# Two more weight slots for the mixture of experts, selection matrices in a ring of three, and fewer products ahead of the routing's positions

## What is computed

```python
def hier_moe(x, router_grp, router_exp, w1, w3, w2):
    xt = x.reshape(-1, D_MODEL)                         # 320 tokens, D_MODEL = 1024
    gp, gi = lax.top_k(jax.nn.softmax(xt @ router_grp), 1)          # best of 4 groups
    sel = ...                                           # the 8 experts of that group
    ev, ei = lax.top_k(sel, 2)
    ew = jax.nn.softmax(ev) * gp
    eid = gi * EXP_PER_GROUP + ei
    combine = jnp.sum(jax.nn.one_hot(eid, N_EXPERTS) * ew[..., None], axis=1)
    for e in range(N_EXPERTS):                          # 32
        hid = jax.nn.silu(xt @ w1[e]) * (xt @ w3[e])    # FF = 256
        y = y + combine[:, e:e + 1] * (hid @ w2[e])
...
y = rms_norm(h + y, ln_f)
```

## Time and profile before

| | |
|---|---|
| median of 3 executions | 959.48 us (954.65, 959.48, 965.29) |
| profiled execution, its own time | 955.93 us |
| its span | 954.3 us |
| mean granted TensorE clock | 0.905 of full |
| TensorE busy | 790.9 us (83%) |
| HBM read | 211.29 MB |

### The profile page before, as it was taken

How to read it: one execution, slowest core, us unless ns; L and a number is a source line. 1 busy time by engine, 2 the same in 40 slices (tenths; PEclk the granted TensorE clock), 3 DMA queues, 4 the chain that set the end, 5 groups by cost and what they waited for, 6 DMA issues and landing times. The chain is left out here.

```text
span 954.3 us, 20697 instructions
## 1 busy us (share of the span) xinstructions
PE 790.9 (83%) x8699; PEld 473.0 (50%) x8699; DVE 352.6 (37%) x653; ACT 186.6 (20%) x430; POOL 153.7 (16%) x300
## 2 busy tenths in 40 slices
PE   3999799989689799584867776799959987899985
PEld 2445466656466567452544554575454433344421
DVE  2000522359532354275775661021252213231113
ACT  3003122125321210132111232210112110111102
POOL 8200020043400100130235335112000000000000
PEclk9999899979889799597877889699959998999999
DMA  8522222122312122155899999996316999999993
GB/s 323 205 88 89 88 103 89 45 76 88 99 30 68 54 39 81 52 169 180 302 416 419 416 342 410 363 386 247 108 70 279 424 422 426 395 384 421 424 425 144
DMA packets 49110, 219.20 MB, mean 230 GB/s; under 512 B 17615, under 2 KB 22010, under 8 KB 24442
## 3 DMA queue, kind: packets, MB, share of 16 engines
q1 hardware_dynamic: 41856, 186.23, 50.6%
q0 software_dynamic: 6512, 31.48, 8.5%
q10 hardware_dynamic: 650, 0.18, 0.1%
HBM read 211.29 MB, written 6.57 MB: 228 GB/s over the span
## 5 line engine op out<-in xcount | busy, mean ns | idle before, releaser
L226 PE MATMUL bank<-arena 128*128 128x320 f32 x256 | 82.8, 467 | 4.2 <-PEq L112 4.2
L1456 DVE STREAM_TRANSPOSE arena<-arena 128x2048 f32<-128x2048 f32 x32 | 72.1, 2288 | 9.4 <-DMA arena<-in_ck 8.4
L201 POOL DMA_DIRECT2D arena<-in_cv x112 | 57.8, 516 | 105.9 <-PE bank L1719 75.6
L503 PE MATMUL bank<-arena 128*128 128x336 f32 x224 | 70.9, 472 | 4.2 <-DVE arena L649 4.2
L2259 PE MATMUL bank<-arena 128*32 128x512 f32 x512 | 67.3, 610 | 6.8 <-DMA arena<-in_w_exp 6.1
L2448 DVE TENSOR_TENSOR arena<-arena,bank 128x512 f32<-128x512 f32 x40 | 27.5, 688 | 116.3 <-PE bank L2236 113.3
L1719 PE MATMUL bank<-arena 128*16 128x128 f32 x1024 | 41.0, 326 | 33.3 <-DMA arena<-in_cv 18.0
L482 PE MATMUL bank<-arena 128*128 128x512 f32 (+1 forms) x144 | 62.1, 593 | 0.0
L226 PEld LDWEIGHTS bank<-arena 128*128 128x128 f32 x256 | 48.6, 201 | 25.6 <-issue 9.5
L1678 PE MATMUL bank<-arena 32*32 32x512 f32 x1024 | 46.3, 714 | 18.1 <-DVE arena L1456 8.6
L503 PEld LDWEIGHTS bank<-arena 128*128 128x128 f32 x224 | 43.8, 200 | 27.2 <-issue 9.7
(11 more groups left out here) (463 smaller groups left out, 1091.8 us busy)
## 6 DMA issues: line engine op xcount, KB each, us to landing
arena<-in_w_exp SPq DMA_DIRECT2D x99, 1024.0 KB, 20.5
arena<-in_ck SPq DMA_DIRECT2D x128, 256.0 KB, 6.3
arena<-in_cv POOLq DMA_DIRECT2D x112, 256.0 KB, 8.1
arena<-in_w_gate SPq DMA_DIRECT2D x8, 1024.0 KB, 4.8
arena<-in_w_za SPq DMA_DIRECT2D x7, 1024.0 KB, 6.9
arena<-in_w_zb SPq DMA_DIRECT2D x6, 1024.0 KB, 12.8
arena<-in_cv SPq DMA_DIRECT2D x16, 256.0 KB, 3.5
arena<-in_w_proj SPq DMA_DIRECT2D x4, 1024.0 KB, 20.0
```

The source lines that it names most:

```text
L201: eng.dma_start(tile[n:P:4, :], src[bass.ds(page, 1)].rearrange("a (p j) n -> (a p) (j n)", j=4))\
L226: mm = nc.tensor.matmul(bank[b][:, 0:TM], w[:, k, a, :], xnT[:, k, NMETA:T], start=(k == 0), stop=(k == KT - 1))
L503: mm = nc.tensor.matmul(bank[j % 2][:, 0:T], w[:, k, (j % 2) * P:(j % 2 + 1) * P], xnT[:, k, :], start=(k == 0), stop=(k == KT - 1))
L1456: return nc.vector.transpose(kT[b % 2][:, :, 128 * m:128 * m + 128].rearrange("p j (n k) -> p n j k", n=4), slot[m].rearrange("p (n j k) - ...
```

## The change

`gsel` shrinks to three quads, used in turn, and lies elsewhere; what comes free holds two more weight slots, so `FIRST` becomes 18. Places 16 and 17 of the ring are loaded in the merge block, one after the residual rows are written, one after the normalised rows are. The pair and triangle constants move. `select(q + 2)` waits for quad q - 1's gather. The final norm's rows are loaded into the slot of the fourth expert's part 1 of quad 6, behind a wait for that part's use. The counts of tiles 0 and 1 against the triangle are one product of 64 columns, in all five products, and `cnt_ps` is raised behind them; the totals follow into another PSUM bank with a semaphore of their own.

```diff
-        full = [S(f"slot_full{i}") for i in range(SLOTS + 8)]
+        full = [S(f"slot_full{i}") for i in range(SLOTS + 10)]
...
+        FIRST = len(wslot) + 2
...
-        FIRST = len(wslot)
...
-        pair, tri2 = sp6(P), sp6(P)
+        pair, tri2 = arena[:, free_k - 2 * P:free_k - P], arena[:, free_k - P:free_k]
...
-        gcmp = sp7(MAXOV, NE)
+        gcmp = Space(arena, sp7.at, sp7.hi)(MAXOV, NE)
...
+        gsel = Space(arena, mark7, mark_t + NHT * HALF)(3, NT, P)
+        spw = Space(arena, mark7 + 3 * NT * P, tail - SLOT)
+        late16 = spw(SLOT)
+        late17 = arena[:, tail - 2 * SLOT:tail - SLOT]
+        assert spw.at <= tail - 2 * SLOT
+        wslot += [late16, late17]
...
                     expert_load(sp, 0, 1, j)
+                sp.wait_ge(S("h2_sb"), NHT)
+                expert_load(sp, *ring[FIRST - 2])
+                sp.wait_ge(S("x2_ready"), NT)
+                expert_load(sp, *ring[FIRST - 1])
...
-                for i in range(NT):
-                    for k in range(i + 1):
-                        r = slice(0, TROWS[k])
-                        nc.tensor.matmul(bank[7][:, i * NE:(i + 1) * NE],
-                                         (ones if k < i else tri_tok if k < NT - 1 else tri2)[r, :], fe(k)[r, :],
-                                         start=(k == 0), stop=(k == i))
+                cols = lambda i, n=1: bank[7][:, i * NE:(i + n) * NE]
+                both = pick[:, 0:2].rearrange("p i g e -> p (i g e)")
+                last = slice(0, TROWS[NT - 1])
+                nc.tensor.matmul(cols(0, 2), tri_tok, both, start=True, stop=False)
+                nc.tensor.matmul(cols(2), tri2[last, :], fe(2)[last, :], start=False, stop=False)
+                nc.tensor.matmul(cols(1), ones, fe(0), start=False, stop=False)
+                for k in range(NT - 1):
+                    mm = nc.tensor.matmul(cols(2), ones, fe(k), start=False, stop=(k == NT - 2))
+                mm.then_inc(S("cnt_ps"), 1)
                 for k in range(NT):
                     r = slice(0, TROWS[k])
-                    mm = nc.tensor.matmul(bank[7][:, NT * NE:(NT + 1) * NE], ones[r, :], fe(k)[r, :],
+                    mm = nc.tensor.matmul(bank[6][:, 0:NE], ones[r, :], fe(k)[r, :],
                                           start=(k == 0), stop=(k == NT - 1))
-                mm.then_inc(S("cnt_ps"), 1)
+                mm.then_inc(S("tot_ps"), 1)
...
-                ch(nc.vector.tensor_copy(tot, bank[7][:, NT * NE:(NT + 1) * NE]))
+                dve.wait_ge(S("tot_ps"), 1)
+                ch(nc.vector.tensor_copy(tot, bank[6][:, 0:NE]))
...
-        gsel = Space(arena, mark7, mark_t + NHT * HALF)(NQD, NT, P)
...
+        lnf = wslot[load_slot(NQD - 2, 1, QE - 1)]
+        lnf2, lnf3 = lnf[:, 0:DM], lnf[:, DM:DM + HALF]
...
-                sp.dma_start(lnb2, ln_row[2, :].partition_broadcast(P)).then_inc(S("lnf_in"), 16)
+                sp.wait_ge(S(used[1]), NQD - 1)
+                sp.dma_start(lnf2, ln_row[2, :].partition_broadcast(P)).then_inc(S("lnf_in"), 16)
...
-                    gather(xg[:, q % 2], gsel[:, q], "xg_ps")
+                    gather(xg[:, q % 2], gsel[:, q % 3], "xg_ps")
...
                     if q + 2 < NQD:
+                        if q:
+                            dve.wait_ge(S("xg_ps"), 2 * q)
                         select(q + 2)
```

More of the change, by code:

```diff
@@ L1875, in build @@
         mark7 = sp7.at
-        sp7 = Space(arena, free_o - NPAIR * T, free_k)
+        sp7 = Space(arena, free_o - NPAIR * T, free_k - 2 * P)
         ohg, w4, eg = (sp7(NT, NG) for _ in range(3))
@@ L2184, in build @@
         used = ("w13a_used", "w13b_used")
+        assert ring.index((NQD - 2, 1, QE - 1)) + FIRST >= len(ring)
+        lnf = wslot[load_slot(NQD - 2, 1, QE - 1)]
+        lnf2, lnf3 = lnf[:, 0:DM], lnf[:, DM:DM + HALF]
         ybank = (0, 1, 2, 3, 6)
@@ L2202, in _ @@
                                              .rearrange("a p n -> (a p) n")).then_inc(ofull[part], 16)
-                sp.dma_start(lnb2, ln_row[2, :].partition_broadcast(P)).then_inc(S("lnf_in"), 16)
+                sp.wait_ge(S(used[1]), NQD - 1)
+                sp.dma_start(lnf2, ln_row[2, :].partition_broadcast(P)).then_inc(S("lnf_in"), 16)
                 for r, c in ((UP, slice(0, HALF)), (DN, slice(HALF, DM))):
-                    sp.dma_start(lnb3[r, :], ln_row[2, c].partition_broadcast(P // 2)).then_inc(S("lnf_in"), 16)
+                    sp.dma_start(lnf3[r, :], ln_row[2, c].partition_broadcast(P // 2)).then_inc(S("lnf_in"), 16)
                 for i in range(NT - 1):
@@ L2427, in select @@
                     e4 = slice(QE * q, QE * (q + 1))
-                    v = gsel[:, q].rearrange("p i (e s) -> p i e s", e=QE)
+                    v = gsel[:, q % 3].rearrange("p i (e s) -> p i e s", e=QE)
                     ch(nc.vector.tensor_tensor(v, bc(bc(iot[:, 0:CAP], 1, QE), 1, NT), bc(flat(posm, e4), 3, CAP),
@@ L2537, in result @@
                     nc.vector.scalar_tensor_tensor(out=tile_of(x2, i), in0=tile_of(h2, i), scalar=rstd[:, i:i + 1],
-                                                   in1=lnb2 if i < NT - 1 else lnb3, op0=mult, op1=mult)\
+                                                   in1=lnf2 if i < NT - 1 else lnf3, op0=mult, op1=mult)\
                         .then_inc(S("y_ready"), 1)
```

## The result

The changed kernel takes 951.61 us (median of 20 executions, 947.64 to 956.53) against 960.23 for the kernel before, now also measured 20 times. The ratio is 0.991, its 95% interval 0.9893 to 0.9926: 8.6 us less, 7.1 to 10.3. The forecast was 9.8 us less. The profiled execution took 953.16 us, its span is 951.6. TensorE's busy time (791.4 us, 790.9 before) and the bytes read (211.29 MB) are the same and the mean granted clock is nearly so (0.900, 0.905 before); the time came out of waiting.

The account below looks back on a forecast made before the run. The prediction took the moe block to be bound by its stream of weight loads; 4.9 (two loads) + 3.9 (dent) + 1.0 (routing) = 9.8 us off 957.7 gave 948.0 us, range 941 to 958.

Parts of the forecast that it names:

- The bound: Moe block: bound by its stream of 1 MB weight loads, 83 of them, 2.47 us each.
- Two loads, 4.9 us: Places 16 and 17 load during merge, leaving 81 stream loads; overflow pass and stream end come 4.9 us earlier.
- The dent, 3.9 us: Stream at 831 to 846 us, 314 GB/s: 18 slots keep the queue filled; gain 3.9 us, bounds 0 to 3.9.
- The final norm's rows, which I had put at nothing: Wait ahead of these rows near the end: costs nothing, with 10 us of cover before they are needed.
- Routing, 1.0 us: End of merge: five count products and separate totals start the moe block 1.0 us earlier, range 0.5 to 2.0.
- What follows the last landing ... the change alters none of it.: After the last weight load lands: the remaining 18.4 us stay as they were.
- a tail of more than 18.4 us: Sign of a wrong forecast: over 18.4 us after the last landing, the final norm's rows among its releasers.
- The sum: Whole kernel: 4.9 + 3.9 + 1.0 = 9.8 us less, from 957.7 to about 948.0 us.
- A: Rival: the stream's dent stays or moves, a rate near 314 GB/s in 825 to 850; 951.8 us, chance 0.15.
- B: Rival: the stream doesn't get ahead because TensorE bounds quads 1 to 3; about 955 us, chance 0.1.
- E: Rival: the late merge loads are held, for instance until the barrier, the dent still closes; 953 us, chance 0.06.
- D: Rival: TensorE's clock stays at its lower level through the overflow pass; slower, 971 us, chance 0.04.

Follow-up runs that it names:

- slots_only: The changed kernel with the old nine count products under one semaphore, 18 slots kept; 951.95 us, ratio 0.9904.
- late_in_stream: The changed kernel with places 16 and 17 loaded as the first loads of the moe block's stream; 956.28 us, ratio 0.9952.
- warm_merge: The changed kernel with unread products added: seven between last logits and counts, two ahead of the first gather; 948.62 us, ratio 0.9879.
- counts_only: The kernel before with only the five count products and the totals' own bank and semaphore; 958.32 us, ratio 0.9981.
- one_slot: The changed kernel with 17 slots, only place 16 loaded late in the merge; 954.54 us, ratio 0.9928.
- no_final_rows: The changed kernel without the final norm's three row loads and VectorE's wait for them; 946.97 us, ratio 0.9878.
- rows_late: The changed kernel with the final norm's rows issued only when the first half of outputs(7) is done; 948.21 us, ratio 0.9900.
- rows_late_warm_merge: The changed kernel with the final norm's rows issued behind the stream and unread products filling the merge's end; 949.58 us, ratio 0.9896.

## Why the prediction was right, and where its terms were off

*The bound.* Right. Two waits for weights mark the path in both kernels, and taking loads out of the stream moved the end.

*Two loads, 4.9 us.* Right: 82.3 to 77.3 us up to the overflow pass, 5.0; 77.3 in slots_only, 82.6 where the loads were put back.

*The dent, 3.9 us.* Right in its mechanism, too large by 1.2. In the changed kernel's profile the dent closed fully (422 GB/s) and place 65 came in time, yet the last weights came only 2.7 us earlier behind the overflow pass (2.6 to 3.1 in the profiles of the changed kernel, slots_only, late_in_stream and warm_merge). The step that failed is that the bytes made up in the dent all come back at the last landing. About 1.0 us of them is found in the last 8 us, where the DMA engines are without work for 15% of the time instead of 3%. The final norm's rows, which I had put at nothing because nobody waits for them, have part in it: with them behind the stream the stretch is 127.8, 3.6 less than before. But no run takes them out of the kernel before, so whether they cost more here than there is not shown. That with no pause the 16 engines drift apart, and those ahead move rows while the slowest still has weights, is a guess; no view here shows single engines.

*Routing, 1.0 us.* Right: 0.92 in counts_only, by the way given, the totals. In the changed kernel the ten count instructions took 2.66 us instead of my 2.42 (706.89 to 709.55), and that cost nothing, since the totals came last anyway. That the cost goes little by what is streamed does hold: at the lower clock one of the totals' instructions took 401 ns with 32 columns, one of the gather's 421 ns with 128.

*"What follows the last landing ... the change alters none of it."* Wrong by 1.6 us in the profile. TensorE's clock was 0.65 in the stretch 927 to 930 and 0.50 in 930 to 933, and the products behind the landing began at the lower level. All five profiles with more slots, the rows within the stream and no fill there have slow products behind the landing (5.0 to 5.3 us for the 26: changed, slots_only, late_in_stream, one_slot, warm_merge), and none of those without one of the three has (3.6: before, counts_only, no_final_rows, rows_late, rows_late_warm_merge). So in these ten profiles the 1.6 us go with the change. The fall of the clock itself does not: in the profile of the kernel before it was at the lower level from 916 to 920, on 26 products of hidden(7, part 1) that took 5.32 us, and TensorE still stood waiting for the last weights behind them; in no_final_rows it fell and was back half a us before the landing; in one_slot and warm_merge it was at its upper level at the landing and fell within 1 us behind it. What decides is whether the slow spell reaches beyond the last landing. Why it does in these five, and whether it does in every execution, stays open. The pattern of TensorE's work alone doesn't settle it: from 8 to 4 us before the landing no_final_rows is busy for 2.19 us and rows_late for 2.21, and the clock fell in the one and not in the other. I had named a tail of more than 18.4 us as a sign of being wrong, with the rows among its releasers; the tail came, but the rows hold nobody up in it.

*The sum.* 0.9 + 5.0 + 2.7 - 1.6 = 7.0 by these columns, with the second column's scatter 5.6 in the one pair of profiles; the medians of 20 executions say 8.6 (7.1 to 10.3). The forecast's 9.8 is within this interval. One pair of profiles can't say more than that the columns and the medians fit: 7.0 lies at the lower edge of the interval, and how many executions have the slow tail isn't known. That 951.61 lies 3.6 above my 948.0 has two sources: 1.2 us of the gain, and 2.5 us of the starting point, since I began from the middle of four executions, 957.7, and the median of 20 is 960.23.

*Rivals.* A did not come: no stretch near 314 GB/s ahead of the last 5 us. But one_slot shows how near it was, with 274 in 840 to 846. B and E did not: TensorE's waits are still for weights, and the late loads landed by 705.9. D did not: the clock was at its lower level until 720 or so, and the gather at the overflow pass took 5.50 us, 5.69 before. Slightly under 1% was within what I had given 0.45. One reading of the slices was off: the two ahead of the plateau that I meant show 108 and 70 GB/s, and the nearly nothing stands in the earlier trace rows alone.

## What to carry to other kernels

Where a kernel runs behind one stream of loads, count the bytes still to move at the moment the stream starts: each load brought forward into an idle stretch is worth its full transfer time, and a deeper ring bridges a wait in the issuing queue, which is a gain of its own (here 5.0 and 2.7 us). Splitting a semaphore helps only up to the next wait on the same path; look for what the consumer needs last. Then look at what is issued with the last loads but needed later: it can be put behind them (0.85 us at the landing here, in the traces alone).

## What I had not expected of the hardware

An idle stretch filled with products that nobody reads raised the clock for what followed at once (ten count instructions from 2.66 to 1.55 us), but not for a gather 3.4 us after that. Filling waits for data is a poor trade where the landing isn't known to within the fill: 2.6 us lost for 1.5 won, then 1.3 for 1.5. TensorE's clock fell for some us near the end in seven of the ten profiles without a fill there, the kernel before among them, and cost time only where the spell reached beyond the last landing. And loads of 0.75 MB issued behind the last weights still held their landing up by about 0.85 us, though the queue had taken them later.
